# Differential attention on one Trainium2 core: high and low parts of a map's queries share one tile, and the score product takes two matmuls instead of three

## What is computed

```python
s = einsum('bqhcd,bkhcd->bhcqk', q_blk, k[:, :n_k]) * scale     # both maps
s = where(kpos <= qpos, s, -inf)
p = softmax(s, axis=-1)
a = p[:, :, 0] - lam * p[:, :, 1]
o = einsum('bhqk,bkhe->bqhe', a, v[:, :n_k])
o = rms_norm_2(o, sub_gain) * (1.0 - lam_init)
```

## Time and profile before

| | us |
|---|---|
| time before, median of 3 runs | 2929.05 |
| lowest and highest of the 3 | 2924.68, 2933.83 |
| the profiled execution, its own time | 2928.22 |
| its span in the trace | 2926.4 |
| PE busy in that span | 2833.6 (97%) |
| the differential attention's slots, first scores to last (1419 to 1516) | about 97 |

### The profile page before, as it was taken

The page is one execution under the profiler, slowest core; times in us unless marked ns, Lnnn a source line. Parts: engine busy times, 40 slices in busy tenths (PEclk is TensorE's granted clock), DMA queues, the critical chain, the costliest instruction groups (busy, mean ns, idle before and its releaser), DMA issues.

```text
span 2926.4 us, 39107 instructions
## 1 busy us (share of the span) xinstructions
PE 2833.6 (97%) x13399; PEld 2315.3 (79%) x13399; DVE 1744.8 (60%) x2111; ACT 1224.7 (42%) x2067; POOL 1079.0 (37%) x498
## 2 busy tenths in 40 slices
PE   6999999999899999999899999999999999999999
PEld 5767788887677888888667888888888888888887
DVE  7486777775566554668566333557566766644333
ACT  3574432224554322244454222356566665522221
POOL 1312344443213444444324444443412442244443
PEclk9999999999999999999999999999999999999999
DMA  6355263643112333332003333323301321133332
GB/s 218 88 167 193 79 203 98 208 127 105 37 30 79 93 99 95 94 95 87 29 26 97 94 94 95 99 88 91 92 23 53 95 87 30 51 94 94 101 94 93
DMA packets 366140, 278.96 MB, mean 95 GB/s; under 512 B 13618, under 2 KB 321203, under 8 KB 366003
## 3 DMA queue, kind: packets, MB, share of 16 engines
q1 hardware_dynamic: 364752, 276.83, 31.3%
q10 hardware_dynamic: 1251, 0.33, 0.0%
HBM read 275.03 MB, written 2.10 MB: 95 GB/s over the span
## 4 chain that ended last, share of the span: by engine, by line
PE 65%; issue 4%; DVE 2%; ACT 2%; POOL 1%; DMA 0%; POOLq 0%; DVEq 0%; ACTq 0%; SPq 0%
PE banks L1187 13%; PE banks L1182 12%; PE banks L1191 12%; PE banks L1050 6%; PE banks L1056 6%; PE banks L1053 6%; PE banks L1456 2%; PE banks L1023 1%; PE banks L1396 1%; PE banks L1184 1%; POOL w_lo L895 1%; PE banks L1385 0%; PE banks L1091 0%; PE banks L1431 0%; PE banks L1430 0%
## 5 line engine op out<-in xcount | busy, mean ns | idle before, releaser
L895 POOL TENSOR_TENSOR w_lo<-w_raw,w_hi 128x1024 fp32r<-128x1024 f32 (+2 forms) x431 | 1028.3, 2386 | 1693.2 <-ACT w_hi L1704 1692.2
L1704 ACT ACTIVATE w_hi<-w_raw 128x1024 fp32r<-128x1024 f32 (+2 forms) x432 | 447.3, 1035 | 1125.8 <-PE banks L1191 793.2
L1050 PE MATMUL banks<-w_hi,h_hi 128*128 128x512 f32 x960 | 386.4, 402 | 0.1
L1056 PE MATMUL banks<-w_lo,h_hi 128*128 128x512 f32 x960 | 376.7, 392 | 1.5 <-POOL w_lo L895 1.5
L1053 PE MATMUL banks<-w_hi,h_lo 128*128 128x512 f32 x960 | 375.2, 391 | 0.7 <-DVE h_lo L601 0.7
L1182 PE MATMUL banks<-h_hi,w_hi 128*128 128x512 f32 x1280 | 341.8, 395 | 7.1 <-ACT h_hi L1885 4.2
L1187 PE MATMUL banks<-h_lo,w_hi 128*128 128x512 f32 x1280 | 321.3, 391 | 2.4 <-DVE h_lo L601 2.3
L1182 PEld LDWEIGHTS banks<-h_hi,w_hi 128*128 128x128 f32 x1280 | 243.1, 190 | 65.0 <-issue 7.6
L1187 PEld LDWEIGHTS banks<-h_lo,w_hi 128*128 128x128 f32 x1280 | 240.5, 188 | 57.6 <-DVE h_lo L601 8.2
L1191 PE MATMUL banks<-h_hi,w_lo 128*128 128x512 f32 x1152 | 284.5, 389 | 0.0
L1191 PEld LDWEIGHTS banks<-h_hi,w_lo 128*128 128x128 f32 x1152 | 216.3, 188 | 44.9
(11 more groups left out here) (373 smaller groups left out, 4272.8 us busy)
## 6 DMA issues: line engine op xcount, KB each, us to landing
Z<-in_ada_w SPq DMA_DIRECT2D x64, 512.0 KB, 5.2
w_raw<-in_m_w_up SPq DMA_DIRECT2D x64, 512.0 KB, 3.9
w_raw<-in_m_w_down SPq DMA_DIRECT2D x64, 512.0 KB, 3.6
w_raw<-in_kv_w SPq DMA_DIRECT2D x48, 512.0 KB, 3.8
w_raw<-in_ffn_w_gate SPq DMA_DIRECT2D x44, 512.0 KB, 3.7
w_raw<-in_ffn_w_up SPq DMA_DIRECT2D x44, 512.0 KB, 3.6
tmp<-in_ada_w SPq DMA_DIRECT2D x32, 512.0 KB, 4.4
w_raw<-in_ffn_w_down SPq DMA_DIRECT2D x32, 512.0 KB, 3.7
```

What stands on the lines that cost most here:

```text
L895: pool.tensor_tensor(wlo[j][:, 0:n], raw[j][:, 0:n], whi[j][:, 0:n], ALU.subtract).then_inc(s_wlo, 1)
L1050: pe.matmul(t, hh, wh, start=k == 0, stop=False)
L1056: mm = pe.matmul(t, hh, wl, start=False, stop=k == DC - 1)
L1704: act.activation(whi[par][:, 0:kc * P], raw[par][:, 0:kc * P], ACT.Copy).then_inc(s_whi, 1)
```

## The change

For heads 1 to 7 a map c gets a query tile of its own, `q[c]`: the map's own 64 rows hold the high part, the other 64 rows hold the low part of the same queries. `k_hi[c]` now holds the high part of the map's keys in both halves of its rows, and `k_lo[c]` stays as it was, with zeros in the other half. So `q[c] x k_hi[c]` gives high x high + low x high at once, and `q[c] x k_lo[c]` gives high x low: two matmuls instead of three. Head 0 keeps its three.

POOL zeroes half as many half tiles (two and two in place of four and four), and makes six casts of 64 x 512 per head in place of one of 128 x 512 and two of 64 x 512; the last two go from one half of the rows to the other. DVE makes four low parts of 64 x 512 per head in place of one of 128 x 512 and two of 64 x 512; those of the queries go across the halves. `low_q(h + 1, 1)` stands at the first slot, ahead of `low_k(h + 1, 1)`. `scores` waits for POOL's casts as well as for the low parts.

```diff
         def diff_parts(h):
             if h == 0:
                 return first_parts()
-            q_hi, q_lo, k_hi, k_lo = parts("diff")
-            return q_hi[h % 2], q_lo[h % 2], [t[h % 2] for t in k_hi], [t[h % 2] for t in k_lo]
+            q_first, q_second, k_hi, k_lo = parts("diff")
+            return [q_first[h % 2], q_second[h % 2]], None, [t[h % 2] for t in k_hi], [t[h % 2] for t in k_lo]
...
                 pool.wait_ge(gemm, past(last.base + last.n))
-                zero([qk[64:128, 5 * S:6 * S], qk[64:128, 7 * S:8 * S], qk[0:64, 9 * S:10 * S], qk[0:64, 11 * S:12 * S]])
+                zero([qk[64:128, 7 * S:8 * S], qk[0:64, 11 * S:12 * S]])
                 for h in range(1, 8):
                     if h == 2:
-                        zero([qk[64:128, 4 * S:5 * S], qk[64:128, 6 * S:7 * S], qk[0:64, 8 * S:9 * S], qk[0:64, 10 * S:11 * S]])
-                    pool.wait_ge(e["high_parts"], past(3 * h))
+                        zero([qk[64:128, 6 * S:7 * S], qk[0:64, 10 * S:11 * S]])
+                    q, _, k_hi, _ = diff_parts(h)
                     pool.wait_ge(e["scores"], past(NB * (h - 1)))
-                    pool.tensor_copy(q_hi[h % 2], zt(h)).then_inc(e["high_parts"], 1)
-                    for c, (r, t) in enumerate(zip(HALF, k_hi)):
-                        pool.wait_ge(e["high_parts"], past(3 * h + c + 1))
-                        pool.tensor_copy(t[h % 2][r, :], zrows(r, 8 + h)).then_inc(e["high_parts"], 1)
-                    pool.wait_ge(e["high_parts"], past(3 * h + 3))
+                    for c, r in enumerate(HALF):
+                        pool.wait_ge(e["high_parts"], past(6 * h - 3 + 2 * c))
+                        pool.tensor_copy(q[c][r, :], zrows(r, h)).then_inc(e["high_parts"], 1)
+                        pool.wait_ge(e["high_parts"], past(6 * h - 2 + 2 * c))
+                        pool.tensor_copy(k_hi[c][r, :], zrows(r, 8 + h)).then_inc(e["high_parts"], 1)
+                    for c, r in enumerate(HALF):
+                        pool.wait_ge(e["high_parts"], past(6 * h + 1 + c))
+                        pool.tensor_copy(k_hi[c][HALF[1 - c], :], zrows(r, 8 + h)).then_inc(e["high_parts"], 1)
+                    pool.wait_ge(e["high_parts"], past(6 * h + 3))
...
-                    pe.wait_ge(e["low_parts"], past(3 * h + 3))
+                    pe.wait_ge(e["low_parts"], past(4 * h + 3))
+                    pe.wait_ge(e["high_parts"], past(6 * h + 3))
...
                     for c in range(2):
                         z = diff_scores(s, c)[:, 0:n]
+                        qs = (q if h == 0 else q[c])[:, b * P:n]
                         kh, kl = k_hi[c][:, 0:n], k_lo[c][:, 0:n]
-                        pe.matmul(z, qh, kh, start=True, stop=False)
-                        pe.matmul(z, qh, kl, start=False, stop=False)
+                        pe.matmul(z, qs, kh, start=True, stop=False)
+                        if h == 0:
+                            pe.matmul(z, q_lo[:, b * P:n], kh, start=False, stop=False)
                         pe.matmul(z[:, b * P:n], identb[:, :], mask(M_C), start=False, stop=False, skip_group_check=True)
-                        mm = pe.matmul(z, ql, kh, start=False, stop=True)
+                        mm = pe.matmul(z, qs, kl, start=False, stop=True)
...
-                def low_q(h):
-                    q_hi, q_lo, _, _ = diff_parts(h)
-                    dve.wait_ge(e["high_parts"], past(3 * h + 1))
+                def low_q(h, c):
+                    r = HALF[c]
+                    q, _, _, _ = diff_parts(h)
+                    dve.wait_ge(e["high_parts"], past(6 * h - 2 + 2 * c))
                     dve.wait_ge(e["scores"], past(NB * (h - 1)))
-                    dve.tensor_tensor(q_lo, zt(h), q_hi, ALU.subtract).then_inc(e["low_parts"], 1)
+                    dve.tensor_tensor(q[c][HALF[1 - c], :], zrows(r, h), q[c][r, :], ALU.subtract).then_inc(e["low_parts"], 1)
...
                     if s == 0:
-                        low_q(1)
+                        low_q(1, 0)
                         low_k(1, 0)
                     if i == 0 and h < 7:
+                        low_q(h + 1, 1)
                         low_k(h + 1, 1)
                     if i == 1 and h >= 2:
                         sub_norm(h - 2)
                     if i == 2 and h < 6:
-                        low_q(h + 2)
+                        low_q(h + 2, 0)
                     if i == 3 and h < 6:
                         low_k(h + 2, 0)
```

More of the change, by code:

```diff
@@ L860, in diff @@
                 e = df
-                q_hi, _, k_hi, _ = parts("diff")
                 last = next(st for st in panels if st.ends == "diff")
                 pool.wait_ge(gemm, past(last.base + last.n))
-                zero([qk[64:128, 5 * S:6 * S], qk[64:128, 7 * S:8 * S], qk[0:64, 9 * S:10 * S], qk[0:64, 11 * S:12 * S]])
+                zero([qk[64:128, 7 * S:8 * S], qk[0:64, 11 * S:12 * S]])
                 for h in range(1, 8):
                     if h == 2:
-                        zero([qk[64:128, 4 * S:5 * S], qk[64:128, 6 * S:7 * S], qk[0:64, 8 * S:9 * S], qk[0:64, 10 * S:11 * S]])
-                    pool.wait_ge(e["high_parts"], past(3 * h))
+                        zero([qk[64:128, 6 * S:7 * S], qk[0:64, 10 * S:11 * S]])
+                    q, _, k_hi, _ = diff_parts(h)
                     pool.wait_ge(e["scores"], past(NB * (h - 1)))
-                    pool.tensor_copy(q_hi[h % 2], zt(h)).then_inc(e["high_parts"], 1)
-                    for c, (r, t) in enumerate(zip(HALF, k_hi)):
-                        pool.wait_ge(e["high_parts"], past(3 * h + c + 1))
-                        pool.tensor_copy(t[h % 2][r, :], zrows(r, 8 + h)).then_inc(e["high_parts"], 1)
-                    pool.wait_ge(e["high_parts"], past(3 * h + 3))
+                    for c, r in enumerate(HALF):
[7 more added lines that the diff above has]
+                    pool.wait_ge(e["high_parts"], past(6 * h + 3))
             def window():
@@ L1513, in scores @@
                     n = (b + 1) * P
-                    q_hi, q_lo, k_hi, k_lo = diff_parts(h)
-                    pe.wait_ge(e["low_parts"], past(3 * h + 3))
+                    q, q_lo, k_hi, k_lo = diff_parts(h)
+                    pe.wait_ge(e["low_parts"], past(4 * h + 3))
+                    pe.wait_ge(e["high_parts"], past(6 * h + 3))
                     if s in (NB, 2 * NB):
-                        zero_rows_in(4)
+                        zero_rows_in(2)
                     if s in (1, 2):
@@ L1521, in scores @@
                     pe.wait_ge(e["probs"], past(2 * s - 4))
-                    qh, ql = q_hi[:, b * P:n], q_lo[:, b * P:n]
                     for c in range(2):
                         z = diff_scores(s, c)[:, 0:n]
+                        qs = (q if h == 0 else q[c])[:, b * P:n]
                         kh, kl = k_hi[c][:, 0:n], k_lo[c][:, 0:n]
-                        pe.matmul(z, qh, kh, start=True, stop=False)
-                        pe.matmul(z, qh, kl, start=False, stop=False)
+                        pe.matmul(z, qs, kh, start=True, stop=False)
+                        if h == 0:
+                            pe.matmul(z, q_lo[:, b * P:n], kh, start=False, stop=False)
                         pe.matmul(z[:, b * P:n], identb[:, :], mask(M_C), start=False, stop=False, skip_group_check=True)
-                        mm = pe.matmul(z, ql, kh, start=False, stop=True)
+                        mm = pe.matmul(z, qs, kl, start=False, stop=True)
                     mm.then_inc(e["scores"], 1)
@@ L2871, in low_k @@
                     _, _, k_hi, k_lo = diff_parts(h)
-                    dve.wait_ge(e["high_parts"], past(3 * h + 2 + c))
+                    dve.wait_ge(e["high_parts"], past(6 * h - 1 + 2 * c if h else 2 + c))
                     dve.tensor_tensor(k_lo[c][r, :], zrows(r, 8 + h), k_hi[c][r, :], ALU.subtract).then_inc(e["low_parts"], 1)
                 def first_head():
-                    q_hi, _, k_hi, k_lo = diff_parts(0)
+                    q_hi, q_lo, k_hi, k_lo = diff_parts(0)
                     dve.wait_ge(h_take, past(last.tiles))
@@ L2884, in first_head @@
                         dve.tensor_copy(k_hi[c][HALF[c], :], zrows(HALF[c], 8)).then_inc(e["high_parts"], 1)
-                    low_q(0)
+                    dve.wait_ge(e["high_parts"], past(1))
+                    dve.tensor_tensor(q_lo, zt(0), q_hi, ALU.subtract).then_inc(e["low_parts"], 1)
                     for c in range(2):
```

## The result

The changed kernel takes 2934.38 us (median of 12 runs, 2930.53 to 2936.82) against 2929.8 for the kernel before in its 12; the ratio is 1.0018, 95% interval 1.001 to 1.0025. It is 4.6 us slower. That is within the 0.3% that I had called the same, but on the side that I did not forecast and outside my range. The profiled execution took 2936.28 us with a span of 2934.2.

The account below looks back on a forecast made before the run. DVE was taken to pace head 1, a chain through PE and ACT heads 2 to 5, PE heads 6 and 7. 6.34 - 0.4 - 0.4 - 0.3 = 5.2 us saved: 2929.05 to 2923.8, range 2918 to 2931.

Parts of the forecast that it names:

- What DVE gets more: Differential attention, DVE: one more 64 x 512 subtraction per head, 0.72 us; in heads 3 to 5 idle time of 2.00 absorbs it.
- DVE becomes the pace: Rival, heads 2 to 6: every cast meets a DVE instruction, gain only 0.5 us, result 2928.5; chance 0.15.
- All three signs of being wrong: Middle periods staying near 12.3 us, clock column dropping in heads 3 to 5, head 2's scores over 1.5 us later.
- What a removed product is worth: PE's score matmuls: priced by distance to the next start, 0.24 us at 512, 0.17 at 384; 6.34 gross.
- POOL's disturbance: Six casts for three slow DVE running beside them: 0.5 us per head taken, within 0 and 1.20.
- The start: Before head 2: head 1's scores 0.7 us later but not the pace; charged 0.4, within -0.4 and +1.5.
- The other side: Rival, middle heads: thinner matmul work lowers TensorE's clock; single falls 1.3 us each, result 2929, chance 0.08; long fall 0.04.
- The range: Whole kernel: own terms 2920 to 2927 us; with rivals and scatter, 2918 to 2931 holds 8 in 10.
- The removed cover for the weights' low parts: Head 6, POOL: weight subtraction starts 1.1 to 4.3 us later, with 6.3 us of cover; cost 0.
- PE's added wait: PE, score slots: one more long-fulfilled wait per slot; taken as 0, at most 0.08 each of 28, 2.2 us.

Follow-up runs that it names:

- e4: The kernel before, with low_k(.,1) moved from the first slot to the fourth behind sub_low, products and casts unchanged; ratio 0.9999, median 2929.2 us.
- e3: The kernel before, with one more 64 x 512 DVE subtraction at each head's first slot, into a tile nobody reads; ratio 1.002, median 2933.29 us.
- e1: The changed kernel, with low_q(.,1) and low_k(.,1) moved from the first slot to an earlier head's fourth slot, behind sub_low; ratio 1.0002, median 2929.63 us.
- e5: The changed kernel, with each map's first product computed twice in heads 1 to 7, so three products again; ratio 1.0039, median 2938.61 us.
- e6: e1, with the first product of the 256- and 128-wide maps computed twice in heads 1 to 5; ratio 0.9993, median 2927.52 us.
- e7: e6, with POOL's casts of heads 3 to 7 started one slot later; ratio 0.9997, median 2927.57 us.
- e8: e7, with head 1's parts made early by DVE in free tiles and POOL beginning with head 2; ratio 0.9994, median 2925.79 us.
- e9: e8 without the one-slot delay of POOL's casts; ratio 0.9979, median 2923.23 us.
- e10: e9, with the first product of every map in head 1 computed three times; ratio 0.9982, median 2924.21 us.

## Why the prediction was wrong

**The step that failed** is in "What DVE gets more" and in what I charged for it: "DVE then needs 11.63 against 11.59, a draw; I charge 0.1 for each of heads 2 to 5". I set DVE's work of a whole head against the whole period and took its 2.00 us of idle time as cover. The cover was in the fourth slot, behind everything; the work was added in the first, ahead of `sub_norm`, which the next values product needs. That deadline had nothing to spare; it cost 0.12 us per head already (e4). Heads 3 and 4 were to be 0.72 shorter and are 0.73 and 0.71 longer. e3 shows the deadline alone, e1 shows it gone. By my own rivals, "DVE becomes the pace" came nearest (chance 0.15), but with the wrong mechanism: it allowed the gain to shrink to 0.08 per head and never below, because it too counted by the whole period. All three signs of being wrong came: middle heads of 13.1 (even longer than the 12.3 I had named), a clock of 0.88 in head 5, and head 2's scores 1.7 us later.

**The sum against e5**: 1.1 us were charged for DVE's and POOL's work, and e5 measures 8.0. 6.34 were counted for the products, and they gave 3.8, of which the fall in head 5 took 1.07 back.

**What a removed product is worth**: the sizes were right for the loop through PE and ACT (0.79 measured between e4 and e6 for 0.82), and that loop was not last any more. In head 6 the 1.34 counted were 0.99, and 1.26 of added work on DVE stood against them, where 0.3 had been charged (+0.27 in place of -1.04); in head 7 with the rest it was -0.78 in place of -1.34.

**POOL's disturbance**: I took 0.5 per head for all that the added casts stretch, and it was larger. DVE works 11.96 us of a middle head (13.12 less 1.16 idle) where it worked 10.41; less 0.72 for the new subtraction, 0.83 is stretching. 0.34 of it stands in front of `sub_norm` and costs time, the rest stands behind it, where the idle stretch hides it. Even with 0.83 the whole-period sum gives DVE 11.96 and still a gain of 0.45, so this size is not what turned the sign. The Trainium skill's rule on the shared interfaces ("GPSIMD Engine Reference", "Specifications") is borne out in kind: SBUF instructions of DVE were stretched from 0.22 to 0.37, 0.75 to 1.17 and, in e7, 0.68 to 0.98, while those that read PSUM (0.74, 0.69) kept their length.

**The start**: charged 0.4, up to 1.5. It is 1.73 longer with head 1. The first 0.68 is the wait for POOL's last cast, as the prediction had it (0.7). PE's row names DVE, but DVE's last subtraction ended at 1427.17 and POOL's last cast at 1427.64, 0.10 before PE went on (rows of PE, DVE and POOL):

```profile
1427.74 0.47 PE L1530 MATMUL banks<-qk_parts 128*128 128x512 f32 x1 [2.13 <-DVE qk_parts L2879]
```

```profile
1426.18 0.99 DVE L2879 TENSOR_TENSOR qk_parts<-Z,qk_parts 64x512 fp32r<-64x512 f32 x1
```

```profile
1425.67 1.97 POOL L876 CAST qk_parts<-Z 64x512 fp32r<-64x512 f32 x2
```

What failed is that this was held to be hidden behind DVE's pace: DVE's work did not run ahead of it. In head 1 itself DVE is busy 11.65 us in place of 10.69, and the head is 1.05 longer. The clock was 0.67 there, at 1.00 before; e8, e9 and e10 speak against it as the cause.

**The other side**: "TensorE's clock falls in the middle heads" was right as a mechanism, and in part as a size: 1.6 us per fall (1.3 estimated), in 1 of the 3 middle heads. Alone it would not have turned the sign: 5.2 less 1.6 is still a gain, and without head 5's fall the stage is still 3.7 us longer than before.

**The range**: the 2927 given as the slow end of the forecast's own terms does not follow from them. With every charge at its upper end the sum leaves a gain of 0.5 us, 2928.5. The whole range (2918 to 2931) held that, and still ended 3.4 us below the result.

**The removed cover for the weights' low parts** and **PE's added wait** cost nothing that shows: PE did not wait for `w_lo` at the first filling matmuls, and the chain of e1 has no piece for the wait.

What stays open: how much of the start's loss is casts and how much subtractions. e3, with three casts and one more subtraction (which waits there for the last of them), is as long (19.28) as the changed kernel (19.13), so the added casts may not be needed for it; no kernel adds the casts alone.

## What to carry to other kernels

Idle time of an engine says nothing without its place: before adding work to an in-order queue, go through what stands behind it, up to the next instruction that another engine needs, and subtract the two times; a wait of 0.1 us in front of overlapping matmuls was in no list of waits. Matmuls taken out of a stage that PE doesn't pace may cost clock; with a few put into PE's waits, their result overwritten, it stayed up in the middle heads at no cost in time. And try the mended order on the old kernel too: two moves gave the three-product kernel 5.7 us, and left the two-product one, with its padding, no faster than that (2923.23 against 2923.49).

## What the runs showed of the hardware

- The same instructions can run at the upper level of TensorE's clock or partly at the lower: of two heads in a row of the changed kernel one was at 1.00 and took 13.12 us, the next at 0.88 on average and took 14.74. Heads 3 to 5 were below 1.00 in 4 of 9 cases with two products, and in none of 33 with three products or with padding.
- A cast on POOL from one half of the rows to the other costs what one within a half does (in the changed kernel 0.61 at best, 0.95 at most, over 14 casts), and a subtraction on DVE whose output lies in the other half 0.69, as the one in place.
- A cast of 64 x 512 beside DVE's combine or subtraction takes up to 0.95 to 1.14 us in place of 0.61, and the DVE instruction is stretched as well (1.17 in place of 0.75). Beside the maxima, which read PSUM, both kept their length: the first cast below took 0.61 beside maxima of 0.69 (1466.67). Four of the six casts of a head in the changed kernel:

```profile
1466.68 0.61 POOL L871 CAST qk_parts<-Z 64x512 fp32r<-64x512 f32 x1 [8.81 <-PE banks L1534]
...
1468.69 0.96 POOL L873 CAST qk_parts<-Z 64x512 fp32r<-64x512 f32 x1
1469.71 1.28 POOL L876 CAST qk_parts<-Z 64x512 fp32r<-64x512 f32 x2
```
